# A two-block transformer kernel on one core: feed-forwards with the gate and up weights as the stationary operand

## The reference, cut to what matters

```
def swiglu(x, w_gate, w_up, w_down):
    return (jax.nn.silu(x @ w_gate) * (x @ w_up)) @ w_down

for layer in range(DEPTH):
    nw = norm_w[layer]
    f = swiglu(rmsnorm(h, nw[0]), ffn_w_gate[layer, 0], ffn_w_up[layer, 0], ffn_w_down[layer, 0])
    h = h + FFN_RES_SCALE * rmsnorm(f, nw[1])
    ...                                        # mixer: h = h + rmsnorm(m, nw[3])
    f = swiglu(rmsnorm(h, nw[4]), ffn_w_gate[layer, 1], ffn_w_up[layer, 1], ffn_w_down[layer, 1])
    h = h + FFN_RES_SCALE * rmsnorm(f, nw[5])

f = swiglu_2(tokens, ff_w1[k], ff_w3[k], ff_w2[k])       # the dense one of the second block
```

## Time and profile before

| | us |
|---|---|
| median of 3 runs | 2607.17 (2606.31 to 2608.64) |
| profiled execution | 2606.88 |
| its span, first to last instruction | 2605.0 |
| TensorE, products busy | 2578.4 (99%) |
| TensorE, weight loads busy | 2139.0 (82%) |
| VectorE busy | 2002.6 (77%) |
| ScalarE busy | 1685.5 (65%) |

### The profile page before, as it was taken

One profiled execution on the slowest core, in us unless ns is written; L12 is line 12 of the kernel. 1 busy time (PEld: TensorE's weight loads), 2 busy tenths in 40 slices (PEclk: granted clock), 3 DMA queues, 4 the chain that ended last, 5 costly groups with the idle time before them and its releaser, 6 DMA issues.

```text
span 2605.0 us, 35035 instructions
## 1 busy us (share of the span) xinstructions
PE 2578.4 (99%) x12506; PEld 2139.0 (82%) x12506; DVE 2002.6 (77%) x2322; ACT 1685.5 (65%) x2239; POOL 166.2 (6%) x207
## 2 busy tenths in 40 slices
PE   9999999999999999999999999999999999999998
PEld 7888888888888878888678888788888888888886
DVE  5557667778767765564678876899999999999998
ACT  5446664454467875453564444788888888888887
POOL 2000000000000001005210000400000000000020
PEclk9999999999999999999999999999999999999999
DMA  9555237768754349543149885799999999999997
GB/s 323 188 176 194 65 128 262 249 229 314 243 178 154 115 151 343 195 150 129 49 168 334 311 270 157 268 394 390 381 383 372 395 367 390 375 385 376 383 381 289
DMA packets 286860, 690.58 MB, mean 265 GB/s; under 512 B 12756, under 2 KB 25456, under 8 KB 286752
## 3 DMA queue, kind: packets, MB, share of 16 engines
q1 hardware_dynamic: 267648, 619.51, 66.6%
q0 software_dynamic: 19104, 69.62, 7.9%
HBM read 673.34 MB, written 15.75 MB: 265 GB/s over the span
## 4 chain that ended last, share of the span: by engine, by line
PE 93%; ACT 3%; DVE 2%; DMA 1%; issue 1%; POOL 0%; ACTq 0%; DVEq 0%; SPq 0%
PE ps L2679 27%; PE ps L2684 27%; PE ps L2680 27%; PE ps L2759 2%; PE ps L2958 2%; PE ps L3027 1%; ACT w_hi L939 1%; DMA w_raw<-in_moe_w 1%; PE ps L3425 0%; DVE w_lo L1740 0%; PE ps L2720 0%; ACT hp L1378 0%; PE ps L3491 0%; PE ps L3269 0%; PE ps L3519 0%
## 5 line engine op out<-in xcount | busy, mean ns | idle before, releaser
L1740 DVE TENSOR_TENSOR w_lo<-w_raw,w_hi 128x1024 fp32r<-128x1024 f32 x1149 | 1379.1, 1225 | 395.2 <-ACT w_hi L939 370.4
L939 ACT ACTIVATE w_hi<-w_raw 128x1024 fp32r<-128x1024 f32 x1152 | 1201.0, 1057 | 707.4 <-PE ps L2684 697.5
L2679 PE MATMUL ps<-w_hi,act_hi 128*128 128x512 f32 (+2 forms) x3328 | 1287.7, 389 | 4.8 <-ACT scr L1332 1.7
L2680 PE MATMUL ps<-w_hi,act_lo 128*128 128x512 f32 (+2 forms) x3328 | 1269.7, 384 | 0.0
L2684 PE MATMUL ps<-w_lo,act_hi 128*128 128x512 f32 (+2 forms) x3328 | 928.4, 384 | 1.4 <-DVE w_lo L1740 1.3
L2679 PEld LDWEIGHTS ps<-w_hi,act_hi 128*128 128x128 f32 x3328 | 625.7, 188 | 128.4 <-ACT w_hi L939 3.9
L2680 PEld LDWEIGHTS ps<-w_hi,act_lo 128*128 128x128 f32 x3328 | 626.1, 188 | 118.7 <-issue 1.4
L2684 PEld LDWEIGHTS ps<-w_lo,act_hi 128*128 128x128 f32 x3328 | 613.3, 188 | 128.3 <-DVE w_lo L1740 4.3
L1727 DVE SCALAR_TENSOR_TENSOR scr<-scr,small 128x1024 f32<-128x1024 f32 x98 | 125.3, 1279 | 5.5 <-DMA scr<-in_ada_w 5.5
L1872 DVE TENSOR_TENSOR act_lo<-ps,act_hi 128x512 fp32r<-128x512 f32 (+1 forms) x87 | 74.1, 852 | 40.2 <-ACT act_hi L1113 40.2
L1113 ACT ACTIVATE act_hi<-ps 128x512 fp32r<-128x512 f32 (+1 forms) x87 | 62.7, 720 | 62.2 <-PE ps L2958 62.2
(11 more groups left out here) (540 smaller groups left out, 1542.3 us busy)
## 6 DMA issues: line engine op xcount, KB each, us to landing
w_raw<-in_moe_w SPq DMA_DIRECT2D x338, 1024.0 KB, 9.3
scr<-in_ada_w POOLq DMA_DIRECT2D x48, 1024.0 KB, 7.0
w_raw<-in_ffn_w_up SPq DMA_DIRECT2D x44, 1024.0 KB, 5.3
w_raw<-in_ffn_w_down SPq DMA_DIRECT2D x44, 1024.0 KB, 4.9
w_raw<-in_ffn_w_gate SPq DMA_DIRECT2D x43, 1024.0 KB, 5.2
...
```

The source lines that it names most:

```text
L939: act.activation(w_hi[:, split_at(g), 0:c * width], w_raw[:, s % RING, o:o + c * width], ACT.Copy).then_inc(hi_done, 1)
L1740: dve.tensor_tensor(w_lo[:, split_at(g), 0:c * width], w_raw[:, s % RING, o:o + c * width], w_hi[:, split_at(g), 0:c * width].bitcast(F32) ...
L2679: pe.matmul(out_ap, act_hi[:, chunk, cols], whi, start=start, stop=False)
L2680: pe.matmul(out_ap, act_lo[:, chunk, cols], whi, start=False, stop=False)
```

## The change: what it does

In the five feed-forwards the first step stays as it was. Behind it steps have 256 hidden columns, and gate and up change their operands: 128 hidden columns of the weights, for 128 of the model's dimension, are the stationary operand, and the activations move. The high and the low parts of all 256 tokens lie side by side (`acts`), so that one product of 512 columns with `w_hi` gives high x high in the left half of a bank and low activation x high weight in the right half; a second one of 256 columns with `w_lo` adds to the left half. The two halves are summed by copying the right one out (ScalarE) and adding (VectorE). Hidden columns are now on the partitions, as `down` wants them, so nothing is turned behind the first step. `rn` is then a factor of columns: TensorE multiplies ones by a diagonal matrix of `rn` to get it as a row on all partitions, VectorE scales the gate's sum by it; the up part stays unscaled, and `boundary` applies `rn` behind the down products (in the squares and as `rn_half`). A granule of gate or up weights is now all of the model's dimension by 128 hidden columns, read from `w_raw` in pieces of 128. The order of the granules, the windows and the waits is written anew. Lines that only call the new functions are left out:

```
-act_hi = sb("act_hi", [P, 16, TOKENS], F32R)
-act_lo = sb("act_lo", [P, 16, TOKENS], F32R)
+acts = sb("acts", [P, 2, 16, TOKENS], F32R)
+act_hi, act_lo = acts[:, 0], acts[:, 1]
...
+def plan_crossed(wg, wu, wd, ff):
+    m_last = crossed_steps(ff)
+    plan_up(wg, 0, BANK)
+    plan_up(wu, 0, BANK)
+    for m in range(1, m_last + 1):
+        f = BANK + PAIR * (m - 1)
+        plan_up(wg, f, PAIR, False)
+        plan_up(wu, f, PAIR, False)
+        if m == 1:
+            plan_down(wd, 0, BANK)
+        elif m < m_last - 1:
+            plan_down(wd, f - PAIR, PAIR)
+    plan_down(wd, ff - 3 * PAIR, 3 * PAIR)
+def crossed_steps(ff):
+    return (ff - BANK) // PAIR
+def crossed_at(ff, m):
+    last = crossed_steps(ff)
+    return 8 if m == 1 else 16 + 6 * (min(m, last - 1) - 2) + 4 * (m == last)
+def crossed_downs(ff, m):
+    return 4 if m == 1 else 0 if m == crossed_steps(ff) - 1 else 2
+def crossed_slot(m):
+    return 8 + 2 * ((m + 1) % 4)
+def raw_part(g, c, width, o):
+    s = g // 2
+    if slots[s][3]:
+        return w_raw[:, s % RING, o:o + c * width]
+    return w_raw[:, s % RING, 0:SLOT].rearrange("p (c n) -> p c n", c=DC)[:, :, P * (g % 2):P * (g % 2) + P]
+def split_part(x, g, c, width):
+    part = x[:, split_at(g), 0:c * width]
+    return part if slots[g // 2][3] else part.rearrange("p (c n) -> p c n", c=DC)
...
+gate_sum = sg[:, 0:BANK].rearrange("p (f n) -> p f n", f=2)
+gate_silu = sg[:, BANK:2 * BANK].rearrange("p (f n) -> p f n", f=2)
+crossed_hid = hp[:, 0:BANK].rearrange("p (f n) -> p f n", f=2)
+rn_row = hp[:, BANK:BANK + TOKENS]
+rn_diag = xt[:, 1280:1280 + TOKENS]
+rn_half = ms[:, 30:32]
...
-plan_ff(t["ffn_w_gate"][0, 0], t["ffn_w_up"][0, 0], t["ffn_w_down"][0, 0], FF1)
+plan_crossed(t["ffn_w_gate"][0, 0], t["ffn_w_up"][0, 0], t["ffn_w_down"][0, 0], FF1)
...
-SUMS_FIRST = {3: 0, 4: 6, 5: 1}
-SUMS_SECOND = {1: 7, 2: 2, 3: 3, 4: 4, 5: 5}
-SUMS_DENSE = {i + 1: i for i in range(6)}
-CTX_WINDOWS = {2: 0, 3: 1}
-CTX_EVICTED = len(SUMS_FIRST) + len(SUMS_SECOND) + len(CTX_WINDOWS)
+SUMS_FIRST = {6: 0, 8: 6, 9: 1}
+SUMS_SECOND = {2: 7, 4: 2, 6: 3, 8: 4, 9: 5}
+SUMS_DENSE = {2 * i + 2: i for i in range(6)}
+CTX_WINDOWS = {4: 0, 6: 1}
+CTX_EVICTED = 4 + len(SUMS_FIRST) + len(SUMS_SECOND) + len(CTX_WINDOWS)
...
+        if crossed:
+            act.activation(xn[:, tb, :], banks(2 * tb, 2), ACT.Square, scale=rn[:, tb:tb + 1],
+                           accum_out=ssq[:, tb:tb + 1]).then_inc(act_sum, 1)
...
+    def crossed(ff, scaled=False, beside=None):
+        last = crossed_steps(ff)
+        base = gp[0] - 4
+        def crossed_high(m):
+            act.wait_ge(hid_done, n(hid_done))
+            at = crossed_slot(m)
+            act.activation(act_hi[:, at:at + 2, :], crossed_hid, ACT.Copy).then_inc(hhi_done, 1)
+        hi(4)
+        act.wait_ge(gran_used, gp[0] - 4)
+        if scaled:
+            act.wait_ge(rs_done, n(rs_done))
+            for tb in range(TB):
+                ins = act.activation(sg[:, tb * BANK:(tb + 1) * BANK], ps[:, 4 + tb, :], ACT.Silu, scale=rn[:, tb:tb + 1])
+            ins.then_inc(silu_done, 1)
+        else:
+            act.activation(sg[:].rearrange("p (b n) -> p b n", b=TB), ps[:, 4:6, :], ACT.Silu).then_inc(silu_done, 1)
+        hi(2)
+        n(hid_done)
+        act.wait_ge(hid_t, n(hid_t))
+        act.activation(act_hi[:, 8:12, :], banks(6, 2).rearrange("p (c n) -> p c n", c=4), ACT.Copy).then_inc(hhi_done, 1)
+        hi(2)
+        for m in range(1, last + 1):
+            if beside and m % 2 == 0:
+                beside(m // 2)
+            hi(crossed_downs(ff, m))
+            act.wait_ge(gran_used, base + crossed_at(ff, m) + 2)
+            act.activation(gate_sum, ps[:, 4:6, TOKENS:BANK], ACT.Copy).then_inc(silu_done, 1)
+            act.wait_ge(hid_done, n(hid_done))
+            act.activation(gate_silu, gate_sum, ACT.Silu).then_inc(silu_done, 1)
+            hi(2)
+            act.wait_ge(gran_used, base + crossed_at(ff, m) + 4)
+            act.activation(crossed_hid, ps[:, 6:8, TOKENS:BANK], ACT.Copy).then_inc(silu_done, 1)
+            crossed_high(m)
+            hi(2)
+        if beside:
+            beside(len(steps(ff)))
...
+        factor = rn_half[:, tb:tb + 1] if factor is None else factor
...
+    def crossed(ff, scaled=False, beside=None, sums=None, windows=None):
+        last = crossed_steps(ff)
+        def crossed_low(m):
+            dve.wait_ge(hhi_done, n(hhi_done))
+            at = crossed_slot(m)
+            dve.tensor_tensor(act_lo[:, at:at + 2, :], crossed_hid, act_hi[:, at:at + 2, :].bitcast(F32),
+                              ALU.subtract).then_inc(hlo_done, 1)
+        if scaled:
+            for tb in range(TB):
+                dve.tensor_scalar(rn_diag[:, tb * P:(tb + 1) * P], ident, rn[:, tb:tb + 1], None, ALU.mult)
+            dve.tensor_scalar(rn_half, rn[:], 0.5, None, ALU.mult)
+        lo(4)
+        layer[0] = sums
+        lo_ahead(2)
+        dve.wait_ge(silu_done, n(silu_done))
+        dve.wait_ge(gran_used, gp[0])
+        dve.tensor_tensor(hp[:].rearrange("p (b n) -> p b n", b=TB), sg[:].rearrange("p (b n) -> p b n", b=TB),
+                          ps[:, 6:8, :], ALU.mult).then_inc(hid_done, 1)
+        n(hid_done)
+        lo(2)
+        if scaled:
+            dve.wait_ge(mod_tp, n(mod_tp))
+            dve.tensor_copy(rn_row, ps[:, 3, 0:TOKENS]).then_inc(mod_red, 1)
+            dve.wait_ge(mod_red, n(mod_red))
+        dve.wait_ge(hhi_done, n(hhi_done))
+        dve.tensor_tensor(act_lo[:, 8:12, :], banks(6, 2).rearrange("p (c n) -> p c n", c=4),
+                          act_hi[:, 8:12, :].bitcast(F32), ALU.subtract).then_inc(hlo_done, 1)
+        lo(2)
+        for m in range(1, last + 1):
+            if beside and m % 2 == 0:
+                beside(m // 2)
+            lo(crossed_downs(ff, m))
+            dve.wait_ge(silu_done, n(silu_done))
+            if scaled:
+                link(dve.tensor_tensor(gate_sum, ps[:, 4:6, 0:TOKENS], gate_sum, ALU.add))
+                dve.tensor_tensor(gate_sum, gate_sum, bc_mid(rn_row, 2), ALU.mult).then_inc(hid_done, 1)
+            else:
+                dve.tensor_tensor(gate_sum, ps[:, 4:6, 0:TOKENS], gate_sum, ALU.add).then_inc(hid_done, 1)
+            lo(2)
+            dve.wait_ge(silu_done, n(silu_done, 2))
+            link(dve.tensor_tensor(crossed_hid, ps[:, 6:8, 0:TOKENS], crossed_hid, ALU.add))
+            dve.tensor_tensor(crossed_hid, crossed_hid, gate_silu, ALU.mult).then_inc(hid_done, 1)
+            dve.wait_ge(hid_done, n(hid_done, 2))
+            if windows and m in windows:
+                context_columns(windows[m]) if sums is None else column_sums(windows[m])
+                if sums == 1 and windows[m] == MOD_G1 // 8:
+                    next_gate()
+            if m == last:
+                if sums == 1:
+                    mod_columns(1)
+                layer[0] = None
+            lo(1)
+            crossed_low(m)
+            lo(1)
+        if beside:
+            beside(len(steps(ff)))
...
+    def crossed(ff, scaled=False, closing=None, sums=None, windows=None):
+        last = crossed_steps(ff)
+        def crossed_up(bank):
+            g = gp[0]
+            pe.wait_ge(hi_done, g + 1)
+            for k in range(DC):
+                pe.matmul(ps[:, bank, :], w_hi[:, split_at(g), k * P:(k + 1) * P], acts[:, :, k, :], start=k == 0, stop=False)
+            pe.wait_ge(lo_done, g + 1)
+            for k in range(DC):
+                ins = pe.matmul(ps[:, bank, 0:TOKENS], w_lo[:, split_at(g), k * P:(k + 1) * P], act_hi[:, k, :],
+                                start=False, stop=k == DC - 1)
+            ins.then_inc(gran_used, 1)
+            gp[0] += 1
+        up(4, [(0, slice(tb * P, tb * P + P), 6 + tb) for tb in range(TB)])
+        for m in range(1, last + 1):
+            pe.wait_ge(silu_done, n(silu_done, 3) - 1 if m > 1 else n(silu_done))
+            if windows and m - 1 in windows:
+                pe.wait_ge(mod_red, n(mod_red))
+            crossed_up(4)
+            if m == 1:
+                pe.wait_ge(hid_done, n(hid_done))
+                for k in range(4):
+                    for tb in range(TB):
+                        o = (k * TB + tb) * P
+                        ins = pe.transpose(banks(6, 2)[:, o:o + P], hp[:, tb * BANK + k * P:tb * BANK + k * P + P], ident)
+                ins.then_inc(hid_t, 1)
+                if scaled:
+                    pe.wait_ge(boot_later, 16 * LATER)
+                    pe.matmul(ps[:, 3, 0:TOKENS], ones, rn_diag, start=True, stop=True).then_inc(mod_tp, 1)
+            crossed_up(5)
+            if m == 1:
+                pe.wait_ge(hlo_done, n(hlo_done))
+            else:
+                pe.wait_ge(hid_done, n(hid_done, 2))
+            crossed_up(6)
+            crossed_up(7)
+            if windows and m in windows:
+                turn_context(windows[m], 2) if sums is None else turn_sums(sums, windows[m], 2)
+            if m == 1:
```

(24 more changed lines are left out.)

74 lines of the change are left out of this document (37 added, 37 removed).

## The result

The changed kernel takes **2672.2 us** (median of 4 runs, 2669.4 to 2675.6), the kernel before 2607.4 on the same chip: ratio 1.025 with a 95% interval of 1.0233 to 1.0266. The forecast was 2658, with a range of 2624 to 2690, and slower at 0.90. The profiled execution took 2673.1 us, its span 2671.2 where before it was 2605.0: +66.2 us, where the working had +50.8.

A forecast was written before the change was run, and what follows sets the result against it. TensorE was taken to bound the kernel, busy for 99% of the span. The terms -12.2, +11.3, +1.7, +47.7 and +2.3 summed to +50.8 us, giving a forecast of 2658 us, range 2624 to 2690.

The forecast's parts named there:

- rival 1: ScalarE and VectorE keep up, feed-forward waits hidden: 2608 us, chance 0.06; 2595 if constants also come in time, chance 0.04.
- rival 2: Only single waits remain, five feed-forward ends and two windows without down granules; steps don't lag: 2630 us, chance 0.14.
- Rival 3: No wait for constants in the first feed-forward, the rest as forecast: 2645 us, chance 0.12.
- rival 4: Strided reads make the splits w_hi and w_lo 10% longer, +30 us: 2688 us, chance 0.10.
- TensorE's own work: Five feed-forwards: crossed granules +8.0 us, turns saved -21.4, products with the diagonal +1.2, two-part operand 0; sum -12.2 us.
- wait for constants: First feed-forward, about 38 us: the product with the diagonal waits for all 29 late loads, 11.3 us.
- clock behind it: After the pause for constants in the first feed-forward, the clock falls to 1.2 GHz for 3.4 us: +1.7 us.
- waits in the feed-forwards: TensorE waits for ScalarE and VectorE by a hand-written schedule: 2.8, 17.0, 12.3, 2.8, 12.8, together 47.7 us.
- late products: The product behind each of 26 waits comes 0.09 us late, as behind turns: +2.3 us.
- Step (a): End of every feed-forward: TensorE waits 2.8 us for hidden's low part, queued behind another granule's w_lo.
- Step (b): Steps with sums: 18.0 us against TensorE's 16.5, so +1.5 per step after the lead, +1.3 with a window's reductions.
- Step (c): Windows of sums, including step 8 without down granules: waits of 4.1 and 4.8 us in the second feed-forward.

The follow-up runs named there:

- e3_nosums: Changed kernel with each of the 112 modulation sums taken over 8 elements in place of 1024: 2629.6 us, ratio 1.0079.
- b_nosums: Kernel before the change with each of the same 112 sums taken over 8 elements in place of 1024: 2607.9 us, ratio 0.9998.
- e8: Changed kernel with splits reordered, ones load counted apart, and step 8's sum window moved to step 7 in second and third feed-forward: 2604.6 us, ratio 0.9991.
- e7: Changed kernel with splits reordered, ones load counted apart, and modulation sums cut to 8 elements each: 2608.9 us, ratio 1.0001.
- e5_order: Changed kernel with the same ScalarE and VectorE instructions, splits queued in another order in the feed-forward steps: 2622.1 us, ratio 1.0051.

## Why the prediction came out right, point by point

**The sign and its reason** were right: rivals 1 and 2 need VectorE to keep up, and e3_nosums shows that its sums decide 43 us, while b_nosums shows them free before. Against rival 2 the trace of the changed kernel speaks directly: the five ends and the two windows without down granules are 18 of the 42.7 us of waits, and the other 25 lie in steps with sums. Rival 3 fell with the 9.7 us wait, rival 4 with the splits' unchanged 1054 and 1224 ns.

**The size** is 14 us below what was measured (15.4 by the spans), inside the forecast's range but at its edge, 2672. The terms of the sum:

| term | forecast | measured | from |
|---|---|---|---|
| TensorE's own work | -12.2 | -8.1 to -8.8 | the five in e8 and in e7, waits and slow clock taken out |
| wait for constants | 11.3 | 9.7 | waits of after |
| clock behind it | 1.7 | 1.9 | 3.8 us with products at 1.2 GHz, 48.05 to 51.8 |
| waits in the feed-forwards | 47.7 | 42.7 | waits of after |
| late products | 2.3 | 5.6 to 6.3 | the five in after against e8 and e7, likewise |
| clock behind the other waits | 0 | 13.3 | windows of after |

The mis-sized term is **the clock**. The prediction took from the earlier trace rows that 0.6 us without products can be followed by 1.7 us lost, applied it to the constants' wait and left it out behind the others. Six of these 27 were followed by a fall, and the stage after them lost 1.5 us more than before. With the measured terms the sum is +65.1 of the +66.2, and the last 1.1 us are about what TensorE's idle time grew by in the stages that the change doesn't touch.

The row of the late products can be read off the third feed-forward, which has eight waits and no fall of the clock. TensorE is busy there (second number) for 1.9 us more than in the trace of e8_window7, which does the same work without a wait: 0.24 us per wait, not 0.09. The changed kernel, then e8_window7:

```profile
590.94:794.40 203.46, 191.94 (x1003) 162.99 (x1002) 160.11 (x191) 99.79 (x136) 9.15 (x13) 1.00 0.69 236
```
```profile
558.84:748.88 190.04, 190.04 (x1004) 163.11 (x1003) 160.72 (x192) 102.13 (x136) 9.15 (x13) 1.00 0.75 253
```

Most of that is no lateness but how a gap is read. A product's row ends 0.165 us after the next one could have started, by the prediction's own figures, so a gap between two rows is 0.165 shorter than the delay, and 0.165 + 0.09 is about what is found. As an estimate, 27 x 0.165 = 4.5 us belong to the waits: 47.2 in place of 42.7, where the schedule by hand had 47.7.

The errors hardly cancel: 13.3 us of clock and 3 to 4 of own work on one side, 1.6 us too much for the constants on the other. The waits themselves were well sized. The upper end of the forecast's own range came from the durations of the two engines, which did not change, and not from the clock; that it reaches as far as the measured 2672 is luck.

**Own work.** The +8.0 for crossed granules had 2.775 us each, from rows in which products of one width follow each other. Behind a crossed granule the next takes 2.79, and a down granule 2.75 (102.28 to 105.03 in the trace of e7_order_ones_nosums) in place of 2.72: 36 x 0.015 + 9 x 0.03 = 0.8 us per feed-forward of 2816, 1.1 in the fifth, 4.3 in all at most; 3.4 to 4.1 were measured. (The prediction's aside "about +2" should be +1.4, 576 more products times its 2.5 ns; the forecast's sum does not use it.) The -21.4 of the turns was not measured apart from it. The lack of a cost for the two-part operand was right.

**Step (a), the ends**, was sized 2.8 each (14.0) and measured 2.3, 3.05, 0.9, 2.7 and 1.85 (10.8).

**Step (b)**: by it every step past the lead costs 1.5 us, and a window's reductions 1.3 more; between the two windows at 652.76 and 690.84 in the third feed-forward lie two steps with 3.5 us of waits, where the schedule has 2 x 1.5 + 1.3 = 4.3. Its sign that VectorE would be "nearly without gaps" did not come, and by its own words gaps in the sum steps would speak for rival 1 or 2: VectorE was busy for 158.7 of 206 us in the second feed-forward, 77%. The sign was drawn wrongly, not the schedule, whose step has two gaps of 1.7 us in 18.0; the trace has 1.64 and 2.07 in the step shown above. VectorE is not full but in the wrong order, and e5_order, which changes nothing else, takes back 50 us. The prediction had the two gaps of 1.7 us per step in its working and didn't draw that conclusion.

**Step (c), windows**, was right in place: the two longest waits in the second feed-forward are 3.9 and 4.7 us where the schedule gave 4.1 and 4.8, and e8_window7 shows that the missing down granules of step 8 are what makes the second of them.
